# Chunk products in four corners of the array, and a conditioning by columns

## The reference, cut to what matters

```python
def rwkv7_scan(r, w, k, v, kk, a):
    def step(S, inp):
        r_t, w_t, k_t, v_t, kk_t, a_t = inp
        sa = jnp.einsum('bhvk,bhk->bhv', S, -kk_t)
        S = (S * w_t[:, :, None, :] + sa[..., None] * (kk_t * a_t)[:, :, None, :]
             + v_t[..., None] * k_t[:, :, None, :])
        y = jnp.einsum('bhvk,bhk->bhv', S, r_t)
        return S, y
```

```python
cond = jax.nn.silu(c) @ w_ada[l] + b_ada[l]          # (1, 1024) @ (1024, 3072)
shift, scale, gate_raw = jnp.split(cond, 3, axis=-1)
h = x * (1.0 + scale[:, None]) + shift[:, None]
```

## Time and profile before

| what | value |
|---|---|
| median of 3 runs | 1913.19 us (1912.94 to 1916.48) |
| the profiled execution | 1914.83 us, its span 1913.0 us |
| PE busy | 1826.5 us (95%), 14714 matmul records |
| DVE busy | 1101.1 us (58%) |
| ACT busy | 816.8 us (43%) |
| POOL busy | 702.3 us (37%) |
| DMA | 193.24 MB, mean 101 GB/s |
| instruction queue | 116 packets, 1.90 MB |

### The profile page before, as it was taken

The page is one execution under the profiler, slowest core; times in us unless marked ns, Lnnn a source line. Parts: engine busy times, 40 slices in busy tenths (PEclk is TensorE's granted clock), DMA queues, the critical chain, the costliest instruction groups (busy, mean ns, idle before and its releaser), DMA issues.

```text
span 1913.0 us, 35599 instructions
## 1 busy us (share of the span) xinstructions
PE 1826.5 (95%) x14714; PEld 1453.3 (76%) x14714; DVE 1101.1 (58%) x1431; ACT 816.8 (43%) x1173; POOL 702.3 (37%) x488
## 2 busy tenths in 40 slices
PE   7999999999998999999999997899998999999996
PEld 4778877899775877777899784775676888888875
DVE  7775787633455118787633453658845446546454
ACT  2343645533533443755533534345724324323332
POOL 2454433210252435643210251333453435343332
PEclk9998999999998999999999999999998999999998
DMA  9782222200431522222200432322143322222222
GB/s 366 237 258 71 88 95 93 80 26 4 166 99 44 172 83 83 88 94 89 84 26 4 166 99 88 143 67 66 56 143 123 108 60 84 67 78 72 71 99 99
DMA packets 63201, 193.24 MB, mean 101 GB/s; under 512 B 5936, under 2 KB 6192, under 8 KB 62672
## 3 DMA queue, kind: packets, MB, share of 16 engines
q1 hardware_dynamic: 63056, 191.10, 30.3%
HBM read 173.25 MB, written 17.83 MB: 100 GB/s over the span
## 4 chain that ended last, share of the span: by engine, by line
PE 62%; issue 21%; DVE 7%; POOL 7%; ACT 2%; DMA 0%; POOLq 0%; SPq 0%; DVEq 0%; ACTq 0%
PE proj L2344 39%; POOL w_lo_sb L719 6%; PE aux L2363 4%; PE aux L2602 3%; DVE slots_sb L1405 2%; PE proj L2602 1%; PE aux L2517 1%; PE aux L2659 1%; DVE area_sb L1405 1%; PE aux L2656 1%; PE aux L2962 1%; PE aux L2968 1%; PE aux L2374 1%; PE aux L2959 1%; DVE slots_sb L1408 1%
## 5 line engine op out<-in xcount | busy, mean ns | idle before, releaser
L719 POOL TENSOR_TENSOR w_lo_sb<-w_raw_sb,w_hi_sb 128x512 fp32r<-128x512 f32 x462 | 684.6, 1503 | 1033.3 <-ACT w_hi_sb L806 1033.2
L2344 PE MATMUL proj<-act_hi_sb,w_hi_sb 128*128 128x512 f32 x1480 | 604.0, 408 | 14.9 <-POOL w_lo_sb L719 3.4
L2344 PE MATMUL proj<-act_hi_sb,w_lo_sb 128*128 128x512 f32 x1480 | 579.3, 391 | 0.0
L2344 PE MATMUL proj<-act_lo_sb,w_hi_sb 128*128 128x512 f32 x1480 | 578.3, 391 | 0.0
L806 ACT ACTIVATE w_hi_sb<-w_raw_sb 128x1024 fp32r<-128x1024 f32 x231 | 244.5, 1058 | 673.0 <-PE proj L2344 516.2
L2344 PEld LDWEIGHTS proj<-act_hi_sb,w_hi_sb 128*128 128x128 f32 x1480 | 279.1, 189 | 98.3 <-issue 30.6
L2344 PEld LDWEIGHTS proj<-act_lo_sb,w_hi_sb 128*128 128x128 f32 x1480 | 279.4, 189 | 63.0 <-issue 8.9
L2344 PEld LDWEIGHTS proj<-act_hi_sb,w_lo_sb 128*128 128x128 f32 x1480 | 278.9, 188 | 60.1
L2363 PE MATMUL aux<-act_hi_sb,w_hi_sb 128*128 128x512 f32 x336 | 137.7, 410 | 23.3 <-issue 18.2
L1405 DVE TENSOR_TENSOR area_sb<-area_sb 128x256 f32<-128x256 f32 (+1 forms) x180 | 117.7, 698 | 44.4 <-PE aux L2518 28.2
L2363 PE MATMUL aux<-act_lo_sb,w_hi_sb 128*128 128x512 f32 x336 | 133.5, 397 | 0.0
(11 more groups left out here) (310 smaller groups left out, 2557.8 us busy)
## 6 DMA issues: line engine op xcount, KB each, us to landing
w_raw_sb<-wall SPq DMA_DIRECT2D x231, 512.0 KB, 3.6
area_sb<-w_ada SPq DMA_DIRECT2D x32, 512.0 KB, 4.5
slots_sb<-w_ada SPq DMA_DIRECT2D x32, 256.0 KB, 6.9
gate_scr<-stage_sb SPq DMA_DIRECT2D x32, 256.0 KB, 2.2
area_sb<-gate_scr SPq DMA_DIRECT2D x8, 1024.0 KB, 9.7
x_scr<-area_sb SPq DMA_DIRECT2D x3, 2048.0 KB, 7.7
area_sb<-x_scr SPq DMA_DIRECT2D x2, 2048.0 KB, 13.5
area_sb<-lru_gates SPq DMA_DIRECT2D x1, 3584.0 KB, 11.7
```

The source lines that it names most:

```text
L719: nc.gpsimd.tensor_tensor(w_lo[:, b % 2, :, :].rearrange("p k n -> p (k n)")[:, half], w_raw[:, b % 2, half], w_hi[:, b % 2, :, :].rearran ...
L2344: ins = MM(bank, w[:, s, k, :], a[:, t, :], start=(start and i == 0), stop=(stop and i == len(terms) - 1))
```

## The change

**Corners.** `halves_of` goes, and `beside` interleaves up to two products. The second may be "across": rows q of the array, columns 1 - q. So two products of two chunks, in two banks, take four different 64x64 corners. z and x of level 0 are both straight (no corner is across), and single products take two corners as before. x and its transpose xt become jobs of their own with banks of their own, and ACT takes each by a copy of 256 columns. The next pair's scores (`sl`, `sb`) are made at the end of the pair before. `end_state` is split from `next_state` on DVE. The second addend of a right side and of an output of odd chunks is in another corner than the first, and waits for it (`rhs_state`, `y_old`). The closing makes keys' and state's parts before the updates are there.

**Columns.** PE takes the w_ada tile itself as the stationary operand, 4 x 128 columns, and one column of c as the moving one; the result is four columns. DVE no longer picks and sums; `c_rows` goes. DVE adds 5, 5, 6 and 6 rows and PE streams 3, 3, 2 and 2. The modulation moves from DVE to ACT. `conditioning` runs later in the projection, and DVE's setup work (`forget_bounds`, `unit_rates`) stands between its rows.

```diff
-ADDED, STREAMED = (0, 1, 3, 5, 6), (2, 4, 7)
+ADDED = ((0, 1, 3, 5, 6), (0, 1, 3, 5, 6), (0, 1, 2, 3, 5, 6), (0, 1, 2, 3, 5, 6))
+STREAMED = tuple(tuple(k for k in range(KT) if k not in rows) for rows in ADDED)
...
                 def stream(q):
 
                     x = job_open(pe, ("ada", 0, q))
-                    pe.wait_ge(S("c_spread"), 3)
-                    for i, k in enumerate(STREAMED):
+                    pe.wait_ge(S("c_ready"), 1)
+                    for i, k in enumerate(STREAMED[q]):
                         n = KT * q + k
                         pe.wait_ge(S(f"ada_part{n % 12}"), 16 * (n // 12 + 1))
-                        MM(x, c_rows[:, i, :], ada_part[:, n % 12], start=(i == 0), stop=False)                            .then_inc(S("ada_streamed"), 1)
+                        for j in range(4):
+                            ins = MM(x[:, j:j + 1], ada_part[:, n % 12, P * j:P * j + P], DV["c"][:, k:k + 1],
+                                     start=(i == 0 and j == 0), stop=False)
+                        ins.then_inc(S("ada_streamed"), 1)
...
-                    if l == 0 and k == 0:
+                    if l == 0 and k == 1:
                         condition(1)
+                    if l == 0 and k == 2:
                         stream(2)
-                    if l == 0 and k == 2:
+                    if l == 0 and k == 3:
                         condition(2)
+                    if l == 0 and k == 4:
                         stream(3)
-                    if l == 0 and k == 4:
+                    if l == 0 and k == 5:
                         condition(3)
...
-                def halves_of(name, columns, *products):
-
-                    x = job_open(pe, name)
+                def beside(*parts):
+
                     for j in range(QT):
-                        for i, (a, b) in enumerate(products):
-                            for q in ROWS:
-                                ins = MM(x[q, columns * j:columns * j + columns], a[q, j, :], b(q, j),
-                                         start=(i == 0), stop=(i == len(products) - 1))
-                    job_full(ins, name)
+                        for q in range(2):
+                            last = []
+                            for x, across, a, b, start, stop in parts:
+                                n = x.shape[1] // QT
+                                to = ROWS[1 - q if across else q]
+                                last.append(MM(x[to, n * j:n * j + n], a[ROWS[q], j, :], b(ROWS[q], j),
+                                               start=start and (stop or j == 0), stop=stop and (start or j == QT - 1)))
+                    return last
...
                 def pair(i):
                     n, c = 2 * i + 2, 2 * i
-                    chunk_scores(n)
-                    chunk_scores(n + 1)
-                    right_side(c)
-                    start_inverse(n)
-                    chunk_updates(c)
+                    inverse_level(n, 0)
+                    right_side(c)
                     grow(n, 0)
-                    state_step(c)
+                    chunk_updates(c)
+                    turn_inverse(n, 0)
                     inverse_level(n, 1)
-                    chunk_output(c)
+                    state_step(c)
                     grow(n, 1)
-                    right_side(c + 1)
+
+                    signalled(beside(turned_part(n, 1, 1)), ("xt", l, n + 1, 1))
+                    evacuated_job(pe, ("st", l, c))
+                    right = half_bank(("rhs", l, c + 1))
+                    last = beside(turned_part(n, 1, 0), (right, True, *state_side(c + 1), True, False))
+                    job_full(last[0], ("xt", l, n, 1))
+                    state_added(last[1], c + 1)
+
                     inverse_level(n, 2)
+                    after_state(c + 1)
+                    signalled(beside((right, False, *keyed_side(c + 1), False, True)), ("rhs", l, c + 1))
+                    chunk_output(c)
+                    grow(n, 2)
+                    out = half_bank(("y", l, c + 1))
+                    old_output(c + 1, out)
                     chunk_updates(c + 1)
-                    grow(n, 2)
-                    state_step(c + 1)
+
+                    keys, own = state_parts(c + 1, half_bank(("st", l, c + 1)))
+                    last = beside(turned_part(n, 2, 0), keys)
+                    job_full(last[0], ("xt", l, n, 2))
                     inverse_level(n, 3)
-                    chunk_output(c + 1)
+                    evacuated_job(pe, ("u", l, c + 1))
+                    signalled(beside(turned_part(n, 2, 1), own), ("xt", l, n + 1, 2), ("st", l, c + 1))
+
+                    key_scores(n)
                     grow(n, 3)
...
+                    if n + 2 < RW_CHUNKS:
+                        lower_scores(n + 2)
+                    inverse_level(n, 4)
+                    if n + 2 < RW_CHUNKS:
+                        upper_scores(n + 2)
+                    tokens(n)
+                    turn_inverse(n, 4)
+                    values(n)
```

The new functions `twin`, `inverse_level`, `grow`, `turn_inverse` and `turned_part` all call `beside`: with two parts for z, x and xt of both chunks (xt of levels 1 to 3 one chunk at a time), and for the scores, keys, tokens and values. ACT's side in the pair is now:

```diff
                     take(rhs_sb, ("rhs", l, c))
+                    grown(n, 0)
                     take(u_sb, ("u", l, c))
-                    grown(n, 0)
-                    take_y(c)
+                    turned_inverse(n, 0)
                     grown(n, 1)
+                    turned_inverse(n, 1)
                     take(rhs_sb, ("rhs", l, c + 1))
-                    take(u_sb, ("u", l, c + 1))
                     grown(n, 2)
+                    take_y(c)
+                    take(u_sb, ("u", l, c + 1))
+                    turned_inverse(n, 2)
```

More of the change, by code:

```diff
@@ L222, in job_plan @@
         jobs.add(("hg_square", l, QT - 1), 0)
[L224 to L292, removed]
@@ new lines, in unit_rates @@
+            def unit_rates():
+                for l in range(DEPTH):
+                    lb = t[:, 4 + 4 * l:8 + 4 * l]
+                    chain.done(TS(DV[f"omlb{l}"], lb, -1.0, 1.0, ALU.mult, ALU.add))
+                    chain.done(TS(DV[f"lbf{l}"], lb, 1e-30, None, ALU.max))
+                chain.done(TS(DV["cl"], V("lam"), -1.0, 0.0, ALU.mult, ALU.max))
+                chain.done(tt(DV["cl"], DV["cl"], DV["cl_t"], ALU.add))
+                chain.done(TS(DV["cl"], DV["cl"], -8.0, None, ALU.mult))
+                chain.done(TS(DV["cl_t"], DV["cl"], -1.0, None, ALU.mult))
@@ L1535, in _ @@
+            conditioned_quarter(3)
+            lows_of(3)
             for l in range(DEPTH):
@@ new lines, in inverse_turned, with grow @@
+                def inverse_turned(n, k, e):
+                    return xt_next[e] if k else both(x_one[e])[1]
+                def grow(n, k):
+                    names = [("x", l, n + e, k) for e in range(2)]
+                    parts = []
+                    for e in range(2):
+                        evacuated_job(pe, ("z", l, n + e, k))
+                        if k:
+                            evacuated_job(pe, ("xt", l, n + e, k - 1))
+                        parts.append((job_open(pe, names[e])[:, 256:512], e == 1 and k > 0,
+                                      inverse_turned(n, k, e), of(z_one[k][e]), True, True))
+                        if k == 0:
+                            signalled(beside(parts[e]), names[e])
+                    if k:
+                        signalled(beside(*parts), *names)
@@ L2741, in pair @@
+                    key_scores(n)
                     grow(n, 3)
-                    key_scores(n)
-                    key_scores(n + 1)
-                    inverse_level(n, 4)
-                    for e in range(2):
-                        tokens(n + e)
-                        values(n + e)
-                    grow(n, 4)
+                    keyed, own = output_parts(c + 1, out)
+                    after_old(c + 1)
+                    last = beside(turned_part(n, 3, 0), keyed)
+                    job_full(last[0], ("xt", l, n, 3))
```

482 lines of the change are left out of this document (314 added, 168 removed).

## The result

The changed kernel takes 1905.22 us (median of 6 runs, 1901.1 to 1907.36), the kernel before 1913.49 on the same chip. The ratio is 0.9947, with a 95% interval of 0.9934 to 0.9960: 8 to 13 us faster by the interval, where 28 were forecast. The medians lie 8.3 us apart and the spans of the profiled executions (1903.2 and 1913.0) 9.8.

The account below looks back on a forecast made before the run. PE's work bounds the chunk stage, with instruction fetch to decide after the change: 21.6 us saved over two layers plus 6 from conditioning, 28 in all, gives 1885 us; own range 1868 to 1900, whole range 1848 to 1908.

Parts of the forecast that it names:

- part 3: Chunk stage: 28 instruction blocks at 3.6 us each make it 107.1 us against 117.8, 10.8 less a layer.
- rival B: Chunk stage: four corners no faster than two, or a block costs 4.05 or more; 1905 to 1909 us; chance 0.18.
- Corners: Chunk-stage products: four corners take 29 ns a matmul instead of 58.3, a pair's PE work 17.6 us against 27.7.
- Fetching: PE instructions: the next block's fetch begins only when the one before is entered, so a block takes 3.2 to 4.05 us.
- The prediction's own last sentence: Chunk stages: each 0.1 us in a block's round is 4 us of the sum.
- Rival A: Chunk stage: fetching is hidden and the chain of products and copies decides; 62 us less, 1851 us; chance 0.18.
- Rival D: Chunk-stage pairs: PE with 1 us holes loses its clock; 1949 us, or 1917 to 1930 with some pairs; chance 0.06.
- The chain: Chunk-stage pairs: five inverse levels of products and copies at 3.2 us, plus products between, bind a pair at 20 us.
- The opening: Kernel's start, conditioning by columns: saves 6 us carried to the end, with 8 and 0 as ends.
- The gap at 65: Kernel's start: PE's 1.96 us wait for DVE before 67.45 goes, and the low clock's 1.7 us too.
- the project at 54.45: Kernel's start: this projection can start at 51.95, limited by POOL's weights, 2.5 us sooner.

Follow-up runs that it names:

- two_corners: Changed kernel with every product on the two straight corners, a group's products one after the other (output wrong); 1915.42 us, kernel before beside it 1916.99.
- fetch_tiny: Kernel before plus 1024 one-column bfloat16 matmuls (2048 instructions, 8 blocks) ahead of layer 0's chunk stage; 1947.42 us, 30.4 more than the kernel before.
- onepass_before: Kernel before with all chunk-stage matmuls in one bfloat16 pass, 2 instructions each instead of 4; 1826.09 us.
- opening_only: Kernel before with only the conditioning by columns changed, chunk stage as before; 1910.69 us, ratio 0.9973.
- both_again: The whole changed kernel timed again on another occasion; 1905.02 us, ratio 0.9957 to the kernel before.
- nops_after: Changed kernel with an empty instruction behind each chunk-stage matmul; these never reached the chip, so it repeats the changed kernel; 1905.42 us.

## Where the prediction held and where it failed

The forecast was 28 us, 8 to 13 were measured. The step that failed is a term of part 3: a block of 256 instructions was taken at 3.6 us ("so I take 3.6"), and in the changed kernel it takes 3.9. The mechanism, a lower bound on a block's time that the array's pace doesn't move, was right. That 1905 us still lies within 1848 to 1908 is luck: that range took in rival B, one of whose two conditions is false, while the prediction's own range (1868 to 1900) was missed.

**What bounded the kernel** was read rightly: PE set the stage, at 58.3 ns a matmul, with the instruction fetch close behind. two_corners puts the old pace back and gets the old stage back within 1 us (117.6 and 117.5 against 117.5 and 116.7).

**Corners.** Right. In its fastest blocks the changed kernel starts a record every 18 ns where it was 29, so 64 matmuls take 2.3 us, 36 ns each; the sum behind the 17.6 us for 448 matmuls is 39 ns each. Where a group goes by four, four records start every 0.06 us, 15 ns each, twice the rate of two corners:

```profile
403.25 0.22 PE L2645 MATMUL proj<-area_sb 64*64 64x64 f32 x2
403.25 0.22 PE L2645 MATMUL aux<-area_sb 64*64 64x64 f32 x2
403.31 0.22 PE L2645 MATMUL proj<-area_sb 64*64 64x64 f32 x2
403.31 0.22 PE L2645 MATMUL aux<-area_sb 64*64 64x64 f32 x2
403.37 0.22 PE L2645 MATMUL proj<-area_sb 64*64 64x64 f32 x2
```

The Trainium skill, TensorEngine Tiling (Array Packing), "The Solution", lists 64x64 as four independent tiles. The trace agrees, with 15 ns a record where two corners have 29.

**Fetching.** The mechanism was right and is now shown by itself (fetch_tiny). A block takes 3.73 to 3.74 us with nothing else around (at the half clock), and its fetches are 3.93 and 3.88 us apart on average over the pairs of the changed kernel's two layers. I had argued from two fetches 3.3 us apart and from an average fetch of 1.1 us. One distance says little: in those same pairs single ones run from 3.4 to 4.7 us. And the 1.1 us leave out what lies before a fetch starts and after it has landed, 1.2 to 1.5 us each in the two rounds above. The only two rows that showed the fetch deciding, 4.05 us apart, I called slow ones. With the mean of 3.9 in the prediction's own sum the stage is 21 + 3 x 7.1 x 3.9 + 9.3 = 113.4 us, against 109.7 to 114.3 measured without the half clock. 0.3 us on 21 blocks in two layers is 13 us, most of the 15 to 20 that were missing; the opening's part, below, is 3 more. The prediction's own last sentence had the exchange rate. The sum was wrong in its shares too: with 3.9 it has 2.4 us of gain in the three pairs and 1.9 in the opening of a stage, and the trace has 2 in the pairs and some 3 up to their beginning, which two_corners puts down to the corners.

**Rival A** (fetching is hidden), with the rule of the Trainium skill, Runtime: NRT & Kernel Launch, "Instruction fetch mechanics", that crossing a block boundary is mostly hidden: the runs disagree in the two float32 chunk stages and in fetch_tiny, where the 256 instructions take PE less than the round of 3.7 to 3.9 us. Elsewhere the fetches lie 10 us and more apart, and PE need not stop for them: in 72 to 171 it was busy 99.00 of 99 us.

**Rival B** had the size nearer (1905 to 1909) with "or a block costs 4.05 or more" as one of its two conditions; that its other condition (four corners no faster than two) is false, two_corners and the 15 ns show. The measured time lies in B's range, and its sum (little gain in the pairs, 1 to 2 us a layer in the opening) is nearer to the trace than the likeliest one. The block of 3.9 lies between the 3.6 and the 4.05.

**Rival D** (the clock) is a part of the result. The sentence that it stayed at 1.00 through a closing with 2.1 us idle in 10 was true and no protection: in the first profile the clock was at half in 470 to 477, at the end of the last pair; other runs had such stretches elsewhere in the stage, or none. No profile of the order before has one that begins in a float32 stage. A block's 2.3 us of array work, doubled, is over the fetch's 3.9, so such a stretch should cost, and stages with it were 114.5 us on average against 111.6 without, up to 118.7.

**The chain** of 20 us a pair stayed untested in float32, since the fetch lies above it. onepass_before shows that stages of 68 us exist when instructions halve, so copies and masks alone don't hold it at 90 (68.6 and 74.3 us in the two orders).

**The opening** was taken at -6 and brought 3.1 in the first profile (opening_only 6.3, both_again 2.1, nops_after and two_corners nothing), 3.8 in the mean of the starts above, and 0.27% (5 us) when timed alone. The gap at 65 and the low clock behind it went, as forecast. The 2.5 us for the project at 54.45 did not come: POOL's weights were not what it waited for; the stretch from the first projection's start to the next one's is 33.0 us where it was 26.5. Of the 6.5 us more, 12 matmuls at the lower clock (0.43 us apart for 0.23) are 2.4, the narrow matmuls in it 2.7 (6.2 us in five groups for 3.5 before), and three waits for DVE 1.4. I had put the narrow matmuls in a stretch "where PE is idle 5.8 of 42" and "DMA bounds"; PE is busy 39.4 of 42 there now.

## What to carry to other kernels

Count instructions as well as array time: in these runs a steady stream of PE instructions ran on average no faster than one block of 256 in 3.7 to 3.9 us, which is 64 float32 matmuls of two passes or 128 of one, in both of the sizes that ran here (64x64 and 16x1). Small float32 matmuls at 58 ns each are already at that limit, so array packing gained 3 to 5 per cent of the stage; one-pass matmuls gained more (1905 to 1888 with a fifth of them in one pass, 1830 with all, at a loss of precision). Fewer and larger matmuls should do the same; no run here tried them. And when gaps in a trace are few, take the size of a limit from the rows where it decides, not from the ones where it doesn't.

## What was not expected of the hardware

Runs of records of one block's length with 0.3 to 1.9 us of silence after them, in a stage where the other engines idle for two thirds of the time. Also a clock at half for 72 us on end in the kernel whose PE was the less busy one: with one-pass matmuls the kernel with the better packing was the slower, 74.3 and 72.8 against 68.6 and 68.5 us a stage, and whether the clock or the longer chain of copies did it stays open.
